# A decoder block on one core: up-projection weights of the experts loaded in 4 MB pieces with runs of 32 KB

## The reference, cut to what matters

```
def moe_ffn(h, w_router, b_router, w_up, b_up, w_down, b_down):
    logits = (xt @ w_router + b_router).astype(jnp.float32)
    top_val, top_idx = lax.top_k(logits, TOP_K)
    gate = jax.nn.softmax(top_val, axis=-1)
    ...
    def expert_block(args):
        xb, e = args
        hu = xb @ w_up[e] + b_up[e]                      # [rows, 1024] @ [1024, 2048]
        x_glu = jnp.minimum(hu[:, :D_FF], SWIGLU_LIMIT)
        x_lin = jnp.clip(hu[:, D_FF:], -SWIGLU_LIMIT, SWIGLU_LIMIT)
        act = x_glu * jax.nn.sigmoid(SWIGLU_ALPHA * x_glu) * (x_lin + 1.0)
        return act @ w_down[e] + b_down[e]               # [rows, 1024] @ [1024, 1024]
    ...
    y = jnp.zeros((n_tok, d), h.dtype).at[row_tok].add(yb * row_w[:, None].astype(h.dtype))
```

## Time and profile before

| | |
|---|---|
| median of three runs | 1273.02 us (1272.98 to 1278.16) |
| the profiled execution | 1272.27 us, its span 1270.5 us |
| PE busy | 1159.0 us, 91% |
| DVE, ACT busy | 454.9 us (36%), 240.1 us (19%) |
| loads of up-projection weights | 128, of 2048 KB each, 34.8 us from issue to landing |
| loads of down-projection weights | 65, 63 of them of 2048 KB, 35.3 us from issue to landing |
| chain of waits that ended last | PE 48%, DMA 47% |

### The profile page before, as it was taken

The page is one execution under the profiler, slowest core; times in us unless marked ns, Lnnn a source line. Parts: engine busy times, 40 slices in busy tenths (PEclk is TensorE's granted clock), DMA queues, the critical chain, the costliest instruction groups (busy, mean ns, idle before and its releaser), DMA issues.

```text
span 1270.5 us, 17784 instructions
## 1 busy us (share of the span) xinstructions
PE 1159.0 (91%) x7512; PEld 609.2 (48%) x7513; DVE 454.9 (36%) x775; ACT 240.1 (19%) x335; POOL 11.8 (1%) x31
## 2 busy tenths in 40 slices
PE   8999999999999999888888888888888888888885
PEld 7998988999633343333333333333333333333321
DVE  5664446657532232222222222332222222222324
ACT  5434546543301010100000000000000000000101
POOL 2000000000000000000000000000000000000000
PEclk9999999999999999999999999999999999999998
DMA  9545333367799999999999999999999999999993
GB/s 293 186 177 198 133 133 133 133 260 286 315 426 426 428 428 429 429 428 428 427 429 429 429 428 429 429 429 428 428 428 429 429 429 429 429 429 427 428 428 150
DMA packets 57087, 456.94 MB, mean 360 GB/s; under 512 B 6397, under 2 KB 8585, under 8 KB 32442
## 3 DMA queue, kind: packets, MB, share of 16 engines
q1 hardware_dynamic: 56472, 454.30, 86.4%
q10 hardware_dynamic: 578, 2.10, 0.4%
HBM read 455.34 MB, written 1.05 MB: 359 GB/s over the span
## 4 chain that ended last, share of the span: by engine, by line
PE 48%; DMA 47%; DVE 2%; issue 1%; ACT 1%; SPq 0%; ACTq 0%; DVEq 0%
PE ps L1202 47%; DMA ring<-in_w_up_dram 36%; DMA arena<-in_w_up_dram 11%; DMA arena<-in_ln_w_dram 0%; PE ps L1333 0%; PE ps L1593 0%; ACT w_split L504 0%; PE ps L1531 0%; DVE h_sb L1117 0%; DVE w_split L747 0%; PE ps L1221 0%; DVE h_sb L1196 0%; DVE arena L896 0%; PE ps L1439 0%; PE ps L1430 0%
## 5 line engine op out<-in xcount | busy, mean ns | idle before, releaser
L1202 PE MATMUL ps<-ring,arena 128*64 128x512 f32 x2304 | 516.3, 596 | 66.0 <-DMA ring<-in_w_up_dram 66.0
L1202 PEld LDWEIGHTS ps<-ring,arena 128*64 128x64 f32 x2304 | 158.4, 137 | 394.6 <-issue 265.9
L1202 PE MATMUL ps<-arena 128*64 128x512 f32 (+3 forms) x932 | 203.9, 551 | 24.7 <-DMA arena<-in_w_up_dram 22.5
L1125 DVE TENSOR_SCALAR arena<-ps 128x512 f32<-128x512 f32 x32 | 22.1, 692 | 500.6 <-PE ps L1202 500.6
L747 DVE TENSOR_TENSOR w_split<-ring,w_split 128x2048 fp32r<-128x2048 f32 x48 | 109.9, 2291 | 107.4 <-ACT w_split L504 107.1
L1202 PEld LDWEIGHTS ps<-arena 128*64 128x64 f32 (+2 forms) x932 | 77.2, 146 | 137.4 <-issue 90.0
L1202 PE MATMUL ps<-x_split,w_split 128*128 128x256 f32 x1152 | 141.4, 284 | 0.0
L1202 PEld LDWEIGHTS ps<-x_split,w_split 128*128 128x128 f32 x1152 | 139.4, 192 | 0.6
L684 ACT ACTIVATE arena<-arena 128x512 f32<-128x512 f32 x32 | 20.2, 631 | 563.7 <-DVE arena L1125 563.7
L504 ACT ACTIVATE w_split<-ring 128x2048 fp32r<-128x2048 f32 x48 | 91.6, 1908 | 59.4 <-PE ps L1202 50.0
L1117 DVE TENSOR_TENSOR h_sb<-ps,h_sb 128x512 f32<-128x512 f32 x132 | 84.8, 684 | 2.2 <-PE ps L1202 2.2
(11 more groups left out here) (220 smaller groups left out, 617.2 us busy)
## 6 DMA issues: line engine op xcount, KB each, us to landing
ring<-in_w_up_dram SPq DMA_DIRECT2D x96, 2048.0 KB, 34.8
ring<-in_w_down_dram SPq DMA_DIRECT2D x47, 2048.0 KB, 35.3
arena<-in_w_up_dram SPq DMA_DIRECT2D x32, 2048.0 KB, 34.8
ring<-in_w_in_dram SPq DMA_DIRECT2D x18, 2048.0 KB, 7.8
arena<-in_w_down_dram SPq DMA_DIRECT2D x16, 2048.0 KB, 35.3
ring<-in_w_proj_b_dram SPq DMA_DIRECT2D x2, 2048.0 KB, 8.5
ring<-in_w_out_dram SPq DMA_DIRECT2D x2, 2048.0 KB, 12.8
ring<-in_w_in_dram SPq DMA_DIRECT2D x2, 1024.0 KB, 9.0
```

What stands on the lines that cost most here:

```text
L1125: dve.tensor_scalar(glu_c, ps[0][:, :], LIMIT, None, ALU.min).then_inc(glu_ok, 1)
L1202: return pe.matmul(dst, lhsT, rhs, start=start, stop=stop, skip_group_check=True)
```

## The change

`w_up` is loaded in pieces of 4 MB, four rows (32 KB) for each partition, and `w_down` in pieces of 2 MB as before. The eight places are taken in pairs: pair 0 lies in the arena, pairs 1 to 3 in the ring. One up piece fills a pair and raises `pair_in`; the two down pieces of an expert share a pair, the first raises `pair_in` and the second `odd_in`. SP waits for `chunk_used` once for each 4 MB, for the later of the two places. PE waits once for each pair and then has 32 matmuls; it still counts `chunk_used` twice.

The eight loads of the first two experts' up-projections keep 2 MB pieces (`load_up_half`): each brings two of the four rows of each partition, 16 KB of a run of 32 KB. Expert 1's first half is issued third, ahead of expert 0's last two, since of the ring's places only those of pair 2 are free then. For the arena to hold 32 KB in one stretch, `ob_high`, `xres`, `slots`, `gates`, `selT_f` and `lnf` move to M0; `ob_high` now lies over `oaT`, so ACT waits for `oa_low_ok` before it writes it. The permutation of the features follows: `first_gather` steps by four columns, ACT's scaled copy and `ln2P` are in the order (2, 4).

```diff
+PAIRS = PLACES // 2
+TURN_PAIRS = UNROLL * PER_EXPERT // 2
...
-        chunk_at = [at(T0, CHUNK), at(G0, CHUNK), ring[:, 2, :], ring[:, 0, :], ring[:, 1, :], ring[:, 3, :],
-                    ring[:, 4, :], ring[:, 5, :]]
+        pair_at = [at(G0, 2 * CHUNK)] + [ring[:, 2 * n:2 * n + 2, :].rearrange("p a n -> p (a n)") for n in range(3)]
...
         def load_up(sp, e, c, n):
-            rows = w_up[0, bass.ds(e, 1), c * 256:c * 256 + 256, :]
-            sp.dma_start(chunk_at[n % PLACES], rows.rearrange("e (p s) n -> p (e s n)", s=2))\
-              .then_inc(chunk_in[n % PLACES], 16)
+            rows = w_up[0, bass.ds(e, 1), c * 512:c * 512 + 512, :]
+            sp.dma_start(pair_at[n // 2 % PAIRS], rows.rearrange("e (p s) n -> p (e s n)", s=4))\
+              .then_inc(pair_in[n // 2 % PAIRS], 16)
+
+        def load_up_half(sp, e, c, half, n):
+            rows = w_up[0, e, c * 512:c * 512 + 512, :].rearrange("(p s) n -> p s n", s=4)
+            sp.dma_start(chunk_at(n).rearrange("p (s n) -> p s n", s=2), rows[:, 2 * half:2 * half + 2, :])\
+              .then_inc((odd_in if n % 2 else pair_in)[n // 2 % PAIRS], 16)
...
                 if c == C_WO:
                     sp.wait_ge(proj_done, PROJ_UNITS)
-                    load_up(sp, 0, 2, 2)
+                    load_up_half(sp, 1, 0, 0, 4)
...
             def up_chunks(e, base, n):
-                for c in range(UP_CHUNKS):
-                    sp.wait_ge(chunk_used, base + (n + c - PLACES + 1))
-                    load_up(sp, e, c, n + c)
+                for c in range(UP_CHUNKS // 2):
+                    sp.wait_ge(chunk_used, base + (n + 2 * c + 1 - PLACES + 1))
+                    load_up(sp, e, c, n + 2 * c)
...
                 if u == S_OBT:
+                    act.wait_ge(oa_low_ok, 1)
...
                 for k in tiles:
-                    first = (k // 2) * 2 * P + k % 2
+                    first = (k // 4) * 4 * P + k % 4
...
-                for c in range(UP_CHUNKS):
-                    chunk_landed(i, first + c)
...
-                    for s in range(2):
+                for c in range(UP_CHUNKS // 2):
+                    pair_landed(i, first + 2 * c)
+                    w = pair_at[(first // 2 + c) % PAIRS]
+                    for s in range(4):
+                        if first_of_all and s == 2:
+                            pe.wait_ge(odd_in[c], 16)
...
                         for side in range(2):
                             for half in range(2):
                                 col = (2 * s + side) * D + half * 512
-                                ins = mm(half_bank(side, half), xin[:, m % 2, 2 * c + s, :], w[:, col:col + 512],
-                                         False, c == UP_CHUNKS - 1 and s == 1)
-                    ins.then_inc(chunk_used, 1)
+                                ins = mm(half_bank(side, half), xin[:, m % 2, 4 * c + s, :], w[:, col:col + 512],
+                                         False, c == 1 and s == 3)
+                        if s % 2:
+                            ins.then_inc(chunk_used, 1)
```

More of the change, by code:

```diff
@@ L219, in layer @@
         slot_loaded = [sem(f"slot_loaded{i}") for i in range(RING)]
-        chunk_in = [sem(f"chunk_in{i}") for i in range(PLACES)]
+        pair_in = [sem(f"pair_in{i}") for i in range(PAIRS)]
+        odd_in = [sem(f"odd_in{i}") for i in range(PAIRS)]
         chunk_used = sem("chunk_used")
@@ L656, in _ @@
                 act.wait_ge(h2_rstd, t + 1)
[L657 to L658 removed]
+                act.activation(xs2[:, t, :].rearrange("q (c s p) -> q c s p", c=2, s=4),
+                               h_sb[:, t, :].rearrange("q (c p s) -> q c s p", c=2, s=4), ACT.Copy,
                                scale=rstd[:, t:t + 1]).then_inc(xs2_ok, 1)
@@ L1472, in first_gather @@
                 for k in tiles:
-                    first = (k // 2) * 2 * P + k % 2
+                    first = (k // 4) * 4 * P + k % 4
                     at_col = (k if k < 2 else k - 2) * CAP
-                    ins = mm(ps[4 if k < 2 else 2][:, at_col:at_col + CAP], h_sb[:, t, first:first + 2 * P - 1:2],
+                    ins = mm(ps[4 if k < 2 else 2][:, at_col:at_col + CAP], h_sb[:, t, first:first + 4 * P - 3:4],
                              sel0[:, t, :], t == 0 and k in (0, 2), t == 1)
@@ L1553, in up @@
                     up_bias(m)
-                for c in range(UP_CHUNKS):
-                    chunk_landed(i, first + c)
[L1556 to L1561, removed]
-                    for s in range(2):
+                for c in range(UP_CHUNKS // 2):
[4 more added lines that the diff above has]
+                            pe.wait_ge(odd_in[c], 16)
+                        if first_of_all and s == 2 and c == 0:
+                            for t in range(TT):
+                                ins = mm(ps[3][:, 2 * E:3 * E], ones[:, :], taken_b[:, t, :], t == 0, t == 1)
+                            ins.then_inc(count_ps, 1)
+                            pe.wait_ge(xin_ok, 1)
                         for side in range(2):
@@ L1575, in down @@
                 for d in range(DOWN_CHUNKS):
-                    chunk_landed(i, first + d)
-                    w = chunk_at[(first + d) % PLACES]
+                    if d:
+                        odd_landed(i, first + d, last)
+                    else:
+                        pair_landed(i, first)
+                    w = chunk_at(first + d)
                     for k in range(4):
@@ L1615, in _ @@
             gather()
+            for n in (UP_CHUNKS, UP_CHUNKS + 2):
+                pe.wait_ge(odd_in[n // 2], 16)
             pe.wait_ge(turns_ok, 1)
```

45 lines of the change are left out of this document (25 added, 20 removed).

## The result

| | before | changed |
|---|---|---|
| median | 1272.98 us (5 runs, 1271.49 to 1278.16) | 1278.47 us (5 runs, 1276.32 to 1278.92) |
| ratio | | 1.0038, 95% interval 1.002 to 1.0055 |
| profiled execution | 1272.27 us, span 1270.5 | 1276.32 us, span 1274.6 |
| mean granted PE clock | 0.995 | 0.974 |

I had forecast 1273 us, that is no change. The kernel is slower, by an amount that is clear of its noise; the time lies inside the range, but the forecast had no slowdown in it.

What follows compares the result with a forecast made beforehand. From about 345 us until the last expert, DMA bytes over rate (428 GB/s) were taken as the bound. Terms -4.7 + 0.8 + 0.3 + 3.4 = -0.2 us gave a forecast of 1273 us, range 1267 to 1282.

Steps and rivals of the forecast that it cites:

- The rate: Weight stream of experts 2 to 31: 60 loads with 32 KB runs save run starts, -4.7 us, 428 to about 431 GB/s.
- the faster rival: Weight stream: 32 KB runs beat the line, 439 GB/s giving 1263 us or 434 giving 1270; chance 0.15.
- The stream's start, the gap: DMA queue's restart before the experts: the second pair arrives late, near 365 us, +0.8 us; bounds 0 and 3.
- The low bound: Gap at the stream's restart: 0 us, if the slowest engine, which ends a piece, has a longer backlog.
- The gather's step: PE's first gather reads h_sb by four columns: 16 loads cost 15 ns more each, +0.3 us; bounds 0 and 2.
- The clock at the start: First gather, ahead of the first up-projection: no fall of PE's clock forecast, no term in sum or bounds.
- The steady part: Middle experts: PE waits 2.8 and 1.0 us per expert, DMA stays the bound, cost 0.
- The rival of the clock: Middle: waits drop PE to 1.2 GHz, 1.5 us per fall; two falls fit, a third gives 1294 us; chance 0.03.
- The end: Last expert: the last up landing releases 32 matmuls, not 16, all on the path, +3.4 us.
- The fall that I expected to stay: End, near the last down-projection: PE at 1.2 GHz for 3.5 us as before; -1.5 us if it does not fall.
- The sum: Whole kernel: -4.7 (rate) + 0.8 (gap) + 0.3 (gather) + 3.4 (end) = -0.2 us.
- runs that are cut or read slowly: Two rivals for the stream: 32 KB runs cut, 1277.5 us, chance 0.18; slower reading at 421 GB/s, 1287.5, chance 0.12.

Runs made afterwards that it cites:

- e2: Changed kernel with 4 MB pairs kept, but each partition's 32 KB in two runs of 16 KB and the old row order (gather step two): 1276.55 us, ratio 1.0036.
- e4: Changed kernel with expert 0's weights in the old row order, so the first gather steps by two; all pairs keep 32 KB runs: 1271.61 us, ratio 0.9998.
- e7: Kernel before with the new row order (gather step four, 2 MB pieces), plus a 512-column matmul after every second matmul of the first gather: 1276.39 us.
- e1: Kernel before with only the new row order in 2 MB up pieces, so the first gather steps by four columns: 1278.86 us, ratio 1.0044.
- e6: Kernel before with each matmul of the first gather issued twice, the extra into a bank that nothing reads: 1276.54 us.

## Why the prediction was wrong, step by step

**The rate.** Right in mechanism and size. Forecast -4.7 us from the line through runs of 2 KB and 16 KB; measured by e2 against e4 4.2 us of stream, and 428 to 431 GB/s; over all profiles the streams with longer runs are 2.2 to 4.8 us shorter. The packets say that a run of 32 KB is one, and e2 that it is the runs and not the transfers. The rate neither fell to 421 nor rose to 439; both were the spread of short windows, as the argument against the faster rival said.

**The stream's start, the gap.** Forecast +0.8, measured at most +0.3 (e2's stream against before's). Part of the difference is a misread row: 180 GB/s in 343 to 344 us is 0.42 us at 428, so the bytes begin at about 343.6 and not 343.9, an issue takes 0.9 us and not 1.1 to reach the dry queue, and the gap comes to 0.5. The low bound named a reason for the rest, a longer backlog of the slowest engine; no run shows it.

**The gather's step: the step that failed.** Forecast "16 x 15 = 0.24 us, taken as +0.3; bounds 0 and 2"; measured 3.7 us for the loads (e7) and 1.5 to 3.0 more for the clock. Three things were wrong in one line. I set the 211 ns of a transpose's load with a step of four beside the 196 ns of a matmul's load with a step of two, and these are two kinds: a transpose's load of contiguous columns takes 140 ns in the same trace of before (min/median/max in ns, first and last start):

```profile
L1439 PEld LDWEIGHTS ps<-ident,h_sb x16: 138/140/224, 321.2 to 332.5; 128*128 128x128 f32 x16
```

So the step of four costs a transpose's load half as much again, and a matmul's load went from 196 to 322 at the same level of the clock (e7). Also, I counted the 16 loads directly ahead of the first up-projection, where all 32 lie on the path. And I let the bound stop at those 16. The prediction itself had the spacing, 0.12 us; doubling it for all 32 is 3.7 us, which would have moved the sum to +3.2 and the forecast to about 1276 us.

The Trainium skill has a rule that spoke against this edit, and I did not weigh it: SBUF — State Buffer, "Door 1: The DMA port swizzle", in its note on cachelines, says that SBUF has lines of 16 bytes, that a reader needs two or more hits in a line to run at full rate, and that each access which crosses to a new line pays. By it a step of two float32 columns, two hits a line, is free, and a step of four, one hit, is not. The traces agree in both: at the upper level of the clock 196 ns for step two, 192 for contiguous columns (the loads from `xnT`), 322 for step four. The same note also says that one may stride up to 4 float32 elements for free, and that does not hold here, if a step of four is meant. The runs show the price at these steps and not that lines are its cause; no other step was run.

**The clock at the start.** Not in the sum and not in the bounds: a term put at nothing, worth 1.5 us in the changed kernel's profiles and 3.0 in e1's. I had asked whether PE's waits would bring the clock down in the middle and at the end, and not whether the slowed gather, narrow matmuls only, would do it just ahead of the first up-projection, at the one place where PE has no cover: the queue is dry there, so each us that PE loses moves the whole stream.

**The steady part.** Right: PE waits for landings throughout (compare; what is waited for, us in sum, times, longest us), 65.9 us in 700:

```profile
PE ps L1215 <- DMA ring<-in_w_up_dram: 49.5, 26, 2.6
PE ps L1215 <- DMA arena<-in_w_up_dram: 16.4, 9, 2.6
```

Forecast were two waits an expert, of 2.8 and 1 us. Of the 35, 24 stand ahead of an expert's second pair and are 2.0 to 2.6 us long, and 11 ahead of the first and are 0.9.

The rival of the clock happened in part, where I had written that the clock would stay up: the window's 0.97 says that PE was at the lower level for 6% of the middle, about 42 us. In 13 of the 24 second pairs the up-projection takes 8.6 to 8.8 us for 7.1, behind waits of 2.1 to 2.6 us; the other 11 have waits as long, 2.0 to 2.6, and no fall. Forecast was that two falls an expert would still be hidden; there was about one in two experts, and with 16 KB runs and the same falls (e2) the stream is as long as before's. They cost nothing.

**The end.** The mechanism was right and its size too: 3.5 us between single waits and pairs at the same clock, forecast 3.4. The fall that I expected to stay was absent in both profiles of the changed kernel and present in before's, which gave 1.5 us back in the comparison of profiles, inside the bounds.

**The sum.** -4.6 (the stream, with the gap in it) + 3.7 (loads) + 1.5 (clock at the start) + 3.5 (end) - 1.5 (no fall in the end) + 1.5 (the older delay of PE's start) comes to the +4.1 us of the profiles. The medians are 5.5 to 6 apart. That the time still fell into the range is luck as far as the start goes: the range was made for runs that are cut or read slowly, and neither happened.

## What to carry to other kernels

When a change of layout makes an operand strided, compare its price only with rows of the same kind of instruction, and count every instance up to the next point where the path has slack. Ask first where the bound resource is dry: there a small delay on any engine moves everything behind it, while PE's losses of 1.7 us in the middle vanished. And take the ends apart: the longer runs shortened the stream by about 4 us, and 2 to 3 us of it were left in the whole once the first expert kept its old order and the last its small pieces.

## What the runs showed of the hardware

- A matmul's load of a float32 stationary operand of 128 x 128 takes 192 to 196 ns with contiguous columns or a step of two at the upper level of the clock, and the gather's loads with a step of two follow each other every 117 ns. With a step of four it takes 322 to 328 ns, one every 233 ns, at either level (e7, changed). At the lower level the step of two has little advantage left: one every 217 ns (e6).
- A run of 32 KB goes as one packet. The stream moved at 431 GB/s with two thirds of its bytes in such runs, 428 with runs of 16 KB, with 4 MB and with 2 MB transfers alike.
- PE's clock fell to 1.2 GHz in a stretch of matmuls of 64 columns whose loads the step of four had slowed, for 10.2 us in three profiles and 13.7 in e1's, and by their mean clock in all runs of these kernels. Matmuls of 512 columns between them kept it up (e7, one profile, and 11 of 12 runs by their mean clock).
- In the middle the clock fell in 13 of 24 second pairs, behind waits of PE of 2.1 to 2.6 us, and did not in 11 with waits of 2.0 to 2.6; with waits of at most 1.3 us, before, the window of 700 us has it at 1.00.
- Before itself has a mean clock of 0.991 for 0.995 to 0.997 in 15 of 82 runs, and these take about 6 us longer.
